# Level products of a gated linear attention in pairs of 64 by 64 blocks, in the two column halves of the array

## The chip, the cores and the metric

The kernel is written in Bass for Trainium2 and runs on one core of one chip. The metric is the time of one execution on the device, in microseconds (us); of several runs the median counts. Everything is fp32.

## The reference, cut to what matters

Two layers of an encoder run over 768 tokens (one sequence of 512 and one of 256). Each layer has a gated linear attention branch (4 heads, 128 key channels, 256 value channels each) and a grouped-query attention branch behind one common input projection. The change touches the first branch alone:

```python
def step(S, inp):                      # one chunk of 64 tokens, forward; the backward one is its mirror, strict
    qi, ki, vi, gi = inp
    b = jnp.cumsum(gi, axis=2)
    diff = b[:, :, :, None, :] - b[:, :, None, :, :]
    decay = jnp.exp(jnp.where(mask[None, None, :, :, None], diff, -jnp.inf))
    A = jnp.einsum('bhic,bhjc,bhijc->bhij', qi, ki, decay)
    o = (jnp.einsum('bhij,bhjv->bhiv', A, vi)
         + jnp.einsum('bhic,bhcv->bhiv', qi * jnp.exp(b), S))
```

Over the whole sequence this is one matrix A over pairs of tokens (i, j), in which each entry is a sum over channels of query times key times the product of the gates between j and i, forward above and backward below the diagonal, and then A times the values.

## The kernel before, in words

The kernel does not walk through chunks. It builds A level by level. On level `span` (`LEVELS` = 1, 2, 4, ... 256) the tokens are cut into blocks of `span`; queries and keys carry the product of the gates up to the border of their block, and the product of the two is A for the pairs of tokens that lie in two neighbouring blocks with a common parent. Doubling the span multiplies queries and keys by the totals of their blocks (`doubled`, L1681 to L1697, on VectorE), and `merge_k` (L1053, ScalarE) picks, for each block, the forward or the backward keys into `scaled[:, 4]`.

For one head `gla_levels` of TensorE (L703) runs `GLA_STEPS` = 10 steps. Step 0 is the plain product of queries and keys (the diagonal), step n the level `LEVELS[n - 1]`. On steps 1 to 7 (spans 1 to 64) it issues one matmul for each of the `NT` = 6 tiles of 128 tokens: the 128 channels are contracted, the stationary side is the 128 keys of the tile, and the moving side is the 128 queries of the tile, of which forward and backward rows of `scaled` alternate in runs of `span` (the three-dimensional `view` on L726). The result is a block of 128 by 128 in PSUM, six beside each other in banks 0 and 1. VectorE then copies into `amat` what lies under the level's mask (`collect`, L1700 with `copy_predicated` on L1706); for spans 1 to 32 the mask is zero in the two corners of the tile that join its first 64 tokens with its last 64, because a pair of blocks of these spans is at most 64 tokens wide. Spans 128 and 256 join different tiles and have their own outputs (`aoff1`, `aoff2`).

Around the levels lies other work of TensorE: `background` (L565) takes tiles of the input projection that are due later, one after the other, with three fp32r matmuls each (L584 to L586, 128 stationary, 256 moving columns). `GLA_DONE` says how many tiles are done by the end of which step; they fill the time in which VectorE and ScalarE prepare the next level. TensorE waits on `prod_free` (VectorE has copied the last product), `k_ready` and `q_ready` before each step, and signals `prod` with the last matmul of a step. ScalarE and GpSimd split the weights for the background into a high and a low part (L935, L1425), and SyncE loads them. After the last level `gla_values` multiplies A with the values (L742). Three heads run in a loop and the last one apart, in each of the two layers, so eight heads in all.

Of the kernel before, what the change touches and what calls it, by code (L numbers as in the profile page):

```python
# [40 lines left out]
P = 128  # L41
# [3 lines left out]
TOK = sum(SEQS)  # L45
# [10 lines left out]
GATE_NORM = 16.0  # L56
LEVELS = (1, 2, 4, 8, 16, 32, 64, 128, 256)
NMASK = 7
AH, KVH, DH = 16, 4, 64
GROUP = AH // KVH  # L60
GRID_W, ROPE_THETA = 64, 10000.0
# [269 lines left out]
def trunk(nc, x_prompt, x_sample, norm_g, w_in, w_gate_f, b_gate_f, w_gate_b, b_gate_b, gla_norm_g,  # L331
          q_norm_g, k_norm_g, w_branch_a, w_branch_b, w_out, final_norm_g,
          identity, masks, rope_cos, rope_sin, y_prompt, y_sample):
    def sb(name, shape, offset, dtype=F32):
        return nc.alloc_sbuf_tensor_at(name, shape, dtype, offset=offset)

    def view(t, start, *dims):

        row = 1
        for n in t.shape[1:]:  # L340
            row *= n
        return bass.AP(t, start, [[row, P]] + [list(d) for d in dims])
# [38 lines left out]
    y_out = sb("y_out", [P, NT, D], R_ACT)  # L381
    mask_raw = sb("mask_raw", [P, NMASK, P], R_O + 13 * ROW)

# [3 lines left out]
    scaled = sb("scaled", [P, 5, TOK], R_O + 6 * ROW)  # L387
# [24 lines left out]
    st_qk = sb("st_qk", [P, 4, NSTAT], R_O + 14 * ROW + NTP * 2 * P * 4)  # L412
    g_qk = sb("g_qk", [P, 2, DH], R_S + P * 4 + NMASK * P + 2 * NSTAT * 4)
    rot1 = sb("rot1", [P, HALF], R_T)
# [3 lines left out]
    ident = sb("ident", [P, P], R_S)  # L418
    mask = sb("mask", [P, NMASK, P], R_S + P * 4, U8)
    st = sb("st", [P, 5, NSTAT], R_S + P * 4 + NMASK * P)  # L420
    bg = sb("bg", [P, 2, GH], R_S + P * 4 + NMASK * P + 5 * NSTAT * 4)
    bg_fix = sb("bg_fix", [P, 2], R_S + P * 4 + NMASK * P + 5 * NSTAT * 4 + 32)
    ps = nc.alloc_psum_tensor("ps", [P, 8 * HALF], F32)
# [47 lines left out]
    with nc.Block() as block:  # L471
# [61 lines left out]
        def _(pe):  # L533
            at = Counts("tensor", pe, w_lo_done=RING, drained=8, pt_lo_ready=2, rot2_free=2)
            mm = nc.tensor.matmul
# [29 lines left out]
            def background(start, stop, bank0=BG_BANK, spare=0, ends=False, turned=0):  # L565


                for u in range(start, stop):
                    i, t = divmod(u, NT)
                    k = i % KT  # L570
                    if t == 0:
                        pe.wait_ge(s.w_lo_done, at("w_lo_done"))
                    end = t == NT - 1
                    if i == 0:
                        t = (t + turned) % NT
                    if turned and u == NT - turned:
                        pe.wait_ge(s.drained, at.peek("drained", 0))
                    if k == 0 and t % 2 == 0:
                        pe.wait_ge(s.bg_free, at.peek("bg_free", 1 - 3 * spare))
                        at.skip("bg_free", 1)  # L580
                    out = ps[:, bank0 * HALF + t * BGW:bank0 * HALF + (t + 1) * BGW]
                    tok = slice(t * P, (t + 1) * P)

                    mm(out, act_hi[:, k, tok], w_hi[:, k % RING, 0:BGW], start=(k == 0 and t % 2 == 0), stop=False, skip_group_check=True)  # L584
                    mm(out, act_hi[:, k, tok], w_lo[:, k % RING, 0:BGW], start=False, stop=False, skip_group_check=True)  # L585
                    last = mm(out, act_lo[:, k, tok], w_hi[:, k % RING, 0:BGW], start=False, stop=(k == KT - 1), skip_group_check=True)  # L586
                    if end:
                        last.then_inc(s.w_used, 1)
                    elif ends and k == KT - 1 and t % 2 == 1:
                        last.then_inc(s.bg_done, 1)  # L590
# [103 lines left out]
            def gla_gates():  # L694

                pe.wait_ge(s.gla_fix, at("gla_fix"))
                pe.wait_ge(s.o_read, at("o_read"))
                for d, start, n in ((0, 0, HALF), (0, HALF, TOK - HALF), (1, 0, TOK - HALF), (1, TOK - HALF, HALF)):
                    z = 2 * HALF + d * TOK + start
                    last = mm(ps[:, z:z + n], wg_fix[:, d, :], gl_t[:, start:start + n], start=True, stop=True)  # L700
                last.then_inc(s.gate_ready, 1)

            def gla_levels(h, done, more):  # L703
                for n in range(GLA_STEPS):
                    pe.wait_ge(s.prod_free, at("prod_free"))
                    if n != 1:
                        pe.wait_ge(s.k_ready, at("k_ready"))
                    if n > 0:
                        pe.wait_ge(s.q_ready, at("q_ready"))

                    span = LEVELS[max(n - 1, 0)]
                    if span == 256:
                        for j in range(NTP):
                            i0, of = (2 * P, 0) if j < 2 else (0, 1)
                            last = mm(ps[:, j * 2 * P:(j + 1) * 2 * P], scaled[:, 4, j * P:(j + 1) * P],
                                      scaled[:, of, i0:i0 + 2 * P], start=True, stop=True)
                    else:
                        for j in range(NT):
                            lhs = scaled[:, 4, j * P:(j + 1) * P]
                            if n == 0:  # L720
                                rhs = view(qk_t, h * (2 * TOK) + j * P, (1, P))
                            elif span == 128:
                                i = j ^ 1
                                rhs = scaled[:, j % 2, i * P:(i + 1) * P]
                            else:
                                rhs = view(scaled, TOK + j * P, (2 * span, P // (2 * span)), (span - TOK, 2), (1, span))  # L726
                            last = mm(ps[:, j * P:(j + 1) * P], lhs, rhs, start=True, stop=True)  # L727
                    last.then_inc(s.prod, 1)
                    background(done[n - 1] if n else GLA_FIRST, done[n])
                    if more and n == GATE_STEP:  # L730
                        gla_gates()
# [121 lines left out]
            for layer in range(DEPTH):  # L853
# [19 lines left out]
                with at.repeat(GH - 1, "gla head") as h:  # L873
                    gla_levels(h, GLA_DONE, True)
                    pe.wait_ge(s.gate_used, at("gate_used", 2))
                    gla_values(h)
                gla_levels(GH - 1, GLA_DONE, False)
                gla_values(GH - 1)
                phase_end(pe, at, s.pe_phase, free=True)
# [1143 lines left out]
```

## Time and profile before

| | us |
|---|---|
| median of 3 runs | 1978.19 |
| lowest and highest run | 1978.09, 1978.83 |
| the profiled execution | 1978.54 |
| its span on the core | 1976.7 |
| mean granted clock of TensorE | 0.995 of full speed |

The profile is of one execution. It gives for each engine its instructions with start and duration. The engines are PE (TensorE's matmuls), PEld (TensorE's weight loads, which overlap matmuls), DVE (VectorE), ACT (ScalarE), POOL (GpSimd) and SP (SyncE). Ends of matmuls are modelled, and their records overlap, so that a stretch is best read from the starts. An fp32 matmul appears as two records of PE and two of PEld; an fp32r matmul appears as one of each, although both are labelled f32. "128*128" before a shape is the part of the array that the instruction uses, as rows by columns. L12 is line 12 of the kernel.

### The profile page before, as it was taken

What the parts mean: (1) busy time and instruction counts of PE and PEld (TensorE: products, weight loads), DVE (VectorE), ACT (ScalarE), POOL (GpSimd) and SP (SyncE); (2) the same over time, 40 slices, a digit from 0 to 9 for tenths busy, and PEclk for the clock granted to TensorE, in tenths of its full rate; (3) what the DMA queues carried; (4) which work ended last, traced back from release to release, by engine and by line L of the source; (5) the groups of instructions that cost most, each with busy time, mean ns of one, the idle gap of its engine ahead of it and who ended that gap; (6) DMA issues with size and microseconds to landing.
All of it is one profiled execution on the core that took longest, in us unless ns stands there. A gap on an engine that the chain in (4) does not pass through costs nothing.

```text
span 1976.7 us, 34929 instructions
## 1 busy us (share of the span) xinstructions
PE 1925.5 (97%) x12944; PEld 1783.0 (90%) x12944; DVE 980.1 (50%) x1376; ACT 943.0 (48%) x1891; POOL 674.9 (34%) x688
## 2 busy tenths in 40 slices
PE   7999999999999999999999999999999999999997
PEld 6989999999999998888899899999999999988886
DVE  5113555569755553434250145557696555643334
ACT  4214554533676775523441335555337767753334
POOL 3423122148311222333653322222672221133244
PEclk9999999999999999999999999999999999999999
DMA  5322221432111114332442122225221121261323
GB/s 173 86 56 58 66 74 53 153 98 61 57 46 60 53 50 161 109 123 70 136 105 66 48 67 63 64 72 164 82 60 49 46 67 44 72 197 64 118 92 143
DMA packets 122961, 169.45 MB, mean 86 GB/s; under 512 B 15696, under 2 KB 89296, under 8 KB 122832
## 3 DMA queue, kind: packets, MB, share of 16 engines
q1 hardware_dynamic: 82656, 107.52, 18.9%
q10 hardware_dynamic: 40176, 60.18, 8.9%
q8 instruction: 85, 1.39, 0.3%
q14 instruction: 44, 0.36, 0.1%
HBM read 136.19 MB, written 31.46 MB: 85 GB/s over the span
## 4 chain that ended last, share of the span: by engine, by line
PE 90%; DVE 3%; ACT 2%; issue 1%; ACTq 1%; DMA 1%; POOL 0%; DVEq 0%
PE ps L584 12%; PE ps L585 12%; PE ps L586 12%; PE ps L538 11%; PE ps L540 10%; PE ps L539 10%; PE ps L727 5%; PE ps L742 3%; PE ps L781 3%; PE ps L795 2%; PE ps L668 2%; PE ps L796 2%; PE ps L770 2%; PE ps L771 2%; ACTq L976 1%
## 5 line engine op out<-in xcount | busy, mean ns | idle before, releaser
L1425 POOL TENSOR_TENSOR w_lo<-w_raw,w_hi 128x256 fp32r<-128x256 f32 (+1 forms) x560 | 570.6, 1026 | 1257.8 <-ACT w_hi L935 1256.1
L584 PE MATMUL ps<-w_hi,act_hi 128*128 128x256 f32 x2112 | 609.8, 289 | 1.9 <-issue 1.3
L586 PE MATMUL ps<-w_hi,act_lo 128*128 128x256 f32 x2112 | 597.2, 283 | 0.0
L585 PE MATMUL ps<-w_lo,act_hi 128*128 128x256 f32 x2112 | 597.2, 283 | 0.0
L935 ACT ACTIVATE w_hi<-w_raw 128x256 fp32r<-128x256 f32 (+1 forms) x560 | 273.4, 495 | 512.3 <-PE ps L540 277.3
L584 PEld LDWEIGHTS ps<-w_hi,act_hi 128*128 128x128 f32 x2112 | 404.0, 191 | 7.5 <-issue 4.1
L585 PEld LDWEIGHTS ps<-w_lo,act_hi 128*128 128x128 f32 x2112 | 404.4, 191 | 2.2
L586 PEld LDWEIGHTS ps<-w_hi,act_lo 128*128 128x128 f32 x2112 | 404.1, 191 | 0.0
L1832 DVE TENSOR_REDUCE st<-ps 128x1 f32<-128x512 f32 (+1 forms) x160 | 109.9, 691 | 126.5 <-PE ps L771 125.9
L538 PE MATMUL ps<-w_hi,o_hi 128*128 128x512 f32 x384 | 155.7, 405 | 1.7 <-DVE merged L1754 0.5
L540 PE MATMUL ps<-w_hi,o_lo 128*128 128x512 f32 x384 | 151.0, 393 | 0.0
L539 PE MATMUL ps<-w_lo,o_hi 128*128 128x512 f32 x384 | 150.9, 393 | 0.0
L1058 ACT ACTIVATE scaled<-scaled 128x768 f32<-128x768 f32 x64 | 53.3, 832 | 154.0 <-DVE scaled L1690 154.0
L1144 ACT ACTIVATE pr<-ps,st 128x512 f32<-128x512 f32 (+1 forms) x192 | 117.1, 612 | 11.8 <-DVE st L1832 9.5
L1838 DVE TENSOR_TENSOR pt_lo<-ps,pt_hi 128x512 fp32r<-128x512 f32 x128 | 88.2, 689 | 60.5 <-ACT pt_hi L1154 59.2
L1154 ACT ACTIVATE pt_hi<-ps 128x512 fp32r<-128x512 f32 x128 | 76.5, 598 | 66.6 <-PE ps L796 51.8
L1706 DVE COPY_PREDICATED amat<-mask,ps 128x768 f32<-128x768 uint8 x56 | 58.0, 1036 | 95.8 <-issue 74.4
L727 PE MATMUL ps<-scaled 128*128 128x128 f32 x768 | 102.4, 284 | 2.0 <-issue 2.0
L781 PE MATMUL ps<-ident,pr 128*128 128x128 f32 x640 | 96.7, 273 | 7.7 <-DVE q_hl L1823 6.9
L727 PEld LDWEIGHTS ps<-scaled 128*128 128x128 f32 x768 | 96.9, 192 | 2.6 <-issue 2.3
L538 PEld LDWEIGHTS ps<-w_hi,o_hi 128*128 128x128 f32 x384 | 72.8, 189 | 19.1 <-issue 3.6
L540 PEld LDWEIGHTS ps<-w_hi,o_lo 128*128 128x128 f32 x384 | 72.8, 190 | 15.9
(181 smaller groups left out, 3468.7 us busy)
## 6 DMA issues: line engine op xcount, KB each, us to landing
w_raw<-in_w_in SPq DMA_DIRECT2D x352, 128.0 KB, 2.1
proj<-stg ACTq DMA_DIRECT2D x36, 768.0 KB, 3.4
w_raw<-in_w_in SPq DMA_DIRECT2D x80, 256.0 KB, 2.7
w_raw<-in_w_out SPq DMA_DIRECT2D x64, 256.0 KB, 2.7
w_raw<-in_w_branch_a SPq DMA_DIRECT2D x32, 256.0 KB, 2.8
w_raw<-in_w_branch_b SPq DMA_DIRECT2D x32, 256.0 KB, 2.7
q<-proj ACTq DMA_DIRECT2D x8, 768.0 KB, 4.8
zb<-proj ACTq DMA_DIRECT2D x8, 768.0 KB, 9.9
```

What stands on the lines that cost most here:

```text
L538: mm(out, s_hi, m_hi, start=first, stop=False)
L539: mm(out, s_hi, m_lo, start=False, stop=False)
L540: return mm(out, s_lo, m_hi, start=False, stop=last)
L584: mm(out, act_hi[:, k, tok], w_hi[:, k % RING, 0:BGW], start=(k == 0 and t % 2 == 0), stop=False, skip_group_check=True)
L585: mm(out, act_hi[:, k, tok], w_lo[:, k % RING, 0:BGW], start=False, stop=False, skip_group_check=True)
L586: last = mm(out, act_lo[:, k, tok], w_hi[:, k % RING, 0:BGW], start=False, stop=(k == KT - 1), skip_group_check=True)
L727: last = mm(ps[:, j * P:(j + 1) * P], lhs, rhs, start=True, stop=True)
L781: last = nc.tensor.transpose(bank(pt_bank(n))[:, place * P:(place + 1) * P], pr[:, n % 2, j * P:(j + 1) * P], ident[:])
L935: A(w_hi[:, slot, 0:width], w_raw[:, slot, 0:width], ACT.Copy).then_inc(s.w_hi_done, 1)
L1144: last = A(pr[:, n % 2, i * w:(i + 1) * w], ps[:, n % 2 * HALF + i * w:n % 2 * HALF + (i + 1) * w], ACT.Exp, bias=nmax(n, i), accum_out=de ...
L1425: G.tensor_tensor(w_lo[:, slot, 0:width], w_raw[:, slot, 0:width], w_hi[:, slot, 0:width].bitcast(F32), ALU.subtract).then_inc(s.w_lo_done, 1)
L1832: V.tensor_reduce(out, view_ps(n % 2 * HALF, (HALF // k, k), (1, HALF // k)), AX.X, ALU.max, negate=True).then_inc(s.neg_max, 1)
```

## The change

Steps 1 to 6 (spans 1 to 32) no longer compute whole tiles. For each chunk of 64 tokens they issue one matmul with the chunk's 64 keys as the stationary and its 64 queries as the moving side. The result goes to the 64 partitions of PSUM that belong to the chunk's place in its tile, 0 to 63 for an even chunk and 64 to 127 for an odd one, so that even chunks use the first 64 columns of the array and odd ones the last 64. The two corners that join the chunks are not computed; PSUM keeps there what it held, and the mask leaves it out of `amat`. The signal, the waits, the other steps and all other engines are as before. From here on line numbers of the change are higher by 1 behind the constant, and by 6 behind the new branch.

```diff
@@ -56,6 +56,7 @@
 LEVELS = (1, 2, 4, 8, 16, 32, 64, 128, 256)
 NMASK = 7
+CHUNK = 64
@@ -714,7 +715,7 @@
                                       scaled[:, of, i0:i0 + 2 * P], start=True, stop=True)
-                    else:
+                    elif n == 0 or span >= CHUNK:
                         for j in range(NT):
                             lhs = scaled[:, 4, j * P:(j + 1) * P]
@@ -725,6 +726,11 @@
                                 rhs = view(scaled, TOK + j * P, (2 * span, P // (2 * span)), (span - TOK, 2), (1, span))
                             last = mm(ps[:, j * P:(j + 1) * P], lhs, rhs, start=True, stop=True)
+                    else:
+                        for c in range(0, TOK, CHUNK):
+                            rows = slice(c % P, c % P + CHUNK)
+                            rhs = view(scaled, TOK + c, (2 * span, CHUNK // (2 * span)), (span - TOK, 2), (1, span))
+                            last = mm(ps[rows, c:c + CHUNK], scaled[:, 4, c:c + CHUNK], rhs, start=True, stop=True)
                     last.then_inc(s.prod, 1)
```

In the program of TensorE the six matmuls of such a step become twelve. The rows below are those of step 4 (span 8) in the looped heads, before; REGISTER_ALU is the count for a wait, L700 the gates of the next head:

```order
L700 MATMUL ps<-gl_t,wg_fix 128x512
L705 REGISTER_ALU
L707 REGISTER_ALU
L727 MATMUL ps<-scaled 128x128 x6
L584 MATMUL ps<-w_hi,act_hi 128x256
L585 MATMUL ps<-w_lo,act_hi 128x256
L586 MATMUL ps<-w_hi,act_lo 128x256
```

and the same place now:

```order
L701 MATMUL ps<-gl_t,wg_fix 128x512
L706 REGISTER_ALU
L708 REGISTER_ALU
L733 MATMUL ps<-scaled 64x64 x12
L585 MATMUL ps<-w_hi,act_hi 128x256
L586 MATMUL ps<-w_lo,act_hi 128x256
L587 MATMUL ps<-w_hi,act_lo 128x256
```

Nothing else has moved: the same work stands before and behind the products on TensorE, and every other engine has the same rows with new line numbers.

## Rows read from the trace of the kernel before

**Rows 1.** The page, part 1: busy time, share of the span, instructions of each engine.
```profile
PE 1925.5 (97%) x12944; PEld 1783.0 (90%) x12944; DVE 980.1 (50%) x1376; ACT 943.0 (48%) x1891; POOL 674.9 (34%) x688
```

**Rows 2.** The page, part 4: the chain that ended last, by engine and line.
```profile
PE 90%; DVE 3%; ACT 2%; issue 1%; ACTq 1%; DMA 1%; POOL 0%; DVEq 0%
```

**Rows 3.** Busy time by stretch: the first head of each layer.
```profile
core 0: us, PE busy (x) PEld busy (x) DVE busy (x) ACT busy (x) POOL busy (x), PEclk, DMA share, GB/s
183.00:241.70 58.70, 58.67 (x450) 57.15 (x450) 30.94 (x38) 27.07 (x41) 13.54 (x19) 1.00 0.24 77
1158.00:1216.50 58.50, 58.48 (x450) 56.95 (x448) 30.94 (x38) 26.85 (x40) 13.55 (x19) 1.00 0.25 78
```

**Rows 4.** The chain in order of time, 184 to 209 us: start, us, what.
```profile
184.76 2.00 PE ps L727 x12
190.71 1.45 PE ps L727 x12
196.11 1.34 PE ps L727 x12
...
202.11 1.34 PE ps L727 x12
207.39 1.34 PE ps L727 x12
```

**Rows 5.** Instructions of line 727 on PE and PEld: duration ns min/median/max, start of first and last.
```profile
L727 PEld LDWEIGHTS ps<-scaled x768: 186/192/196, 184.5 to 1374.8; 128*128 128x128 f32 x192
L727 PE MATMUL ps<-scaled x768: 271/275/348, 184.6 to 1374.9; 128*128 128x128 f32 x192
```

**Rows 6.** Timeline of PE, 201 to 203.6 us: start, us, engine, line, operation, tiles.
```profile
201.00 0.28 PE L585 MATMUL ps<-w_lo,act_hi 128*128 128x256 f32 x1
201.12 0.28 PE L586 MATMUL ps<-w_hi,act_lo 128*128 128x256 f32 x1
...
201.95 1.50 PE L727 MATMUL ps<-scaled 128*128 128x128 f32 x12
203.20 0.36 PE L584 MATMUL ps<-w_hi,act_hi 128*128 128x256 f32 x1
203.40 0.28 PE L585 MATMUL ps<-w_lo,act_hi 128*128 128x256 f32 x1
203.52 0.28 PE L586 MATMUL ps<-w_hi,act_lo 128*128 128x256 f32 x1
```

**Rows 7.** Timeline of PE, 227 to 230 us: the products of span 256.
```profile
227.98 1.89 PE L715 MATMUL ps<-scaled 128*128 128x256 f32 x8
```

**Rows 8.** Timeline of PEld, 129.8 to 132.6 us, past a drain in the program.
```profile
130.79 0.19 PEld L538 LDWEIGHTS ps<-w_hi,act_hi 128*128 128x128 f32 x1 [0.65 <-issue]
130.90 0.19 PEld L539 LDWEIGHTS ps<-w_lo,act_hi 128*128 128x128 f32 x1
```

**Rows 9.** Timeline of PE over the same place.
```profile
129.94 0.39 PE L539 MATMUL ps<-w_lo,act_hi 128*128 128x512 f32 x1
130.17 0.39 PE L540 MATMUL ps<-w_hi,act_lo 128*128 128x512 f32 x1
130.82 0.47 PE L538 MATMUL ps<-w_hi,act_hi 128*128 128x512 f32 x1 [0.26 <-DVE va L1920]
```

**Rows 10.** Timeline of PEld, 564.4 us: two weight loads of transposes; then 564.65, one alone.
```profile
564.38 0.20 PEld L781 LDWEIGHTS ps<-ident,pr 128*128 128x128 f32 x2 [0.49 <-ACTq L1146]
564.65 0.14 PEld L781 LDWEIGHTS ps<-ident,pr 128*128 128x128 f32 x1
```

**Rows 11.** Timeline of all engines, 186.9 to 190.6 us, between two levels.
```profile
186.90 1.03 DVE L1706 COPY_PREDICATED amat<-mask,ps 128x768 f32<-128x768 uint8 x1 [2.47 <-PE ps L727]
187.82 0.94 DVE L1690 TENSOR_TENSOR scaled<-scaled,gate 128x768 f32<-128x768 f32 x1
188.80 0.96 ACT L1058 ACTIVATE scaled<-scaled 128x768 f32<-128x768 f32 x1 [4.13 <-DVE scaled L1690]
190.54 0.29 PE L727 MATMUL ps<-scaled 128*128 128x128 f32 x1
```

**Rows 12.** Waits of PE for others, longest first.
```profile
PE ps L727 <- issue: 2.0, 2, 1.2
```

## The prediction

> **What bounds the kernel now.** I read the page's busy times first: the matmuls fill 97% of the span, VectorE 50%, ScalarE 48% [rows 1]. Then the chain that ended last, where TensorE holds 90% [rows 2]. Both say that a saving on TensorE is a saving of time, and an addition an addition. The change lies in one stage, so I asked for that stage by itself: in one head of the linear attention TensorE is busy 58.67 of 58.70 us in the first layer and 58.48 of 58.50 in the second, at the full granted clock, which is the 2.4 GHz level, while VectorE has 31 us of work and ScalarE 27 [rows 3]. In all eight heads together PE stood idle ahead of line 727 for 2.0 us, at two places of 1.2 us at most [rows 12]. So here TensorE is the bound almost to the last nanosecond, and the time that the changed matmuls hold it is what counts.
>
> **What the changed part costs now.** The chain in order of time shows the groups of line 727 of one head: twelve records each, 2.00 us for span 1, 1.45 for span 2, 1.34 for each of spans 4 to 32 [rows 4]; the row for span 32 is like those of 4 to 16. That makes 2.00 + 1.45 + 4 x 1.34 = 8.81 us per head and 70.5 us over eight heads: the most that is at stake. Six matmuls give twelve records, since an fp32 matmul is two.
>
> How long a record holds the engine is read from starts, since its duration of 275 ns [rows 5] is its whole way through the array. The group at 201.95 us lasts 1.50 us; without the last record's 0.275 that leaves 11 spacings, 0.1114 us each [rows 6]. With 256 moving columns (eight records in 1.89 us, the last of them some 0.38 us) the spacing is (1.89 - 0.38) / 7 = 0.216 us [rows 7]. Hence 128 columns cost 0.1046 us and each record a constant 0.0068. Two things run at this pace side by side: the moving columns, and the weight loads. Behind a drain, with nothing in their way, two loads of 128 columns start 0.11 us apart [rows 8]. So both the stream and the loads are at their limit in line 727, and for a gain the change must relieve both.
>
> **The change, part by part.**
>
> 1. *Half the stationary columns, half the moving ones, twice the matmuls.* A group becomes 24 records with 64 moving columns and loads of 64. If they go one after the other, a record takes 0.0523 + 0.0068 = 0.059 us, and a group 24 x 0.059 = 1.42 us in place of 1.34: +0.082 us, times 48 groups (6 steps x 4 heads x 2 layers) **+3.9 us**. The loads alone need half of 0.11 us each, 24 x 0.055 = 1.32 us, so they give the same answer even if the streams of the two halves ran at once. I take this value. What was thrown away was arithmetic, and no row says that the array charges for arithmetic: it charges for columns streamed and columns loaded, and 24 x 64 is 12 x 128. The corners cost moving columns only if the halves really work beside each other; that is the rival.
>
> 2. *Twelve more instruction pairs per group.* Can TensorE issue a matmul and a load every 0.055 us? At 564.38 two loads fill 0.20 us, of which the second takes 0.14, so it starts 0.06 us behind the first, with a matmul issued between them [rows 10]. If 0.06 were the floor, 24 pairs would take 1.44 us, 0.02 over the 1.42; that is +1 us in all. From below the floor costs nothing. I leave it at nothing.
>
> 3. *Switching between the whole array and its halves.* Every group is now entered from matmuls on 128*128 and left for them: 96 switches. The trace of before has none; every record is 128*128. Bounds: below, nothing, since the change from fp32r to fp32 and back at 201.95 leaves no gap: the sequence from 201.95 to the second background matmul at 203.40 is 1.45 us for twelve spacings of 0.1114 and one of 0.12 [rows 6]. Above, the drain that the program itself orders: from the start of L540 at 130.17 to that of L538 at 130.82 is 0.65 us where two of its kind stand 0.23 apart, so 0.42 us for each, part of which is a semaphore [rows 9]; 96 x 0.42 = 40 us. What a switch that only has to let the array run empty would cost lies between: a background matmul lasts 0.28 us and its successor starts 0.12 us behind it, so 0.16 us are its tail [rows 6], which a drain exposes; and if the weight load may not go ahead either, half of 0.11 us on the way in and 0.11 on the way out come on top [rows 8]. That is 2 x 0.16 = 0.32 to 0.49 us per group. I take 0.40, because loads run ahead everywhere else: 48 x 0.40 = **+19.2 us**. The value is nearest to the tail, which is a row, and far from 0, because I suppose that results still on their way through one cut of the array have to leave it before another cut is set.
>
>    The Trainium skill states the rule outright (TensorEngine Tiling (Array Packing), Key Properties): changing the tiling mode drains TensorE, changing only the tile does not. By that rule the 96 switches are paid and the steps from one half to the other inside a group are free; without it the sum would be 3.9 us.
>
> 4. *The other engines.* VectorE's masked copy, its products and ScalarE's `merge_k` are as before. Their chain starts with the product's signal (L1706 at 186.90) and ends at 188.80 + 0.96 = 189.76, while TensorE comes back at 190.54 after a fixed amount of background [rows 11]. That 0.78 us of slack does not depend on how long the group took, so neither a shorter nor a longer group turns into a wait. The one place where TensorE waits 1.2 us in each layer [rows 12] stays or absorbs up to as much, 2 us in all, which I don't count.
>
> Sum: 3.9 + 0 + 19.2 = +23.1 us on the profiled execution's 1978.54, so 2001.6; that execution stands 0.35 us above the median of 1978.19, so against the median **2001.3 us**, 1.2% slower. A measurement of this kernel can tell about 0.2% (4 us) from no change. The forecast's own range comes from the tail alone (3.9 + 15.4: 1997.5) to tails with both loads (3.9 + 23.5: 2005.6), with a little for item 2: 1996 to 2008.
>
> **The rivals.**
>
> *A. The halves work at once, and switches are paid (faster).* If loads and streams of an even and an odd chunk overlap fully, a group takes half of what it takes in item 1: the 70.5 + 3.9 us become 37.2, a saving of 33.3 us. With the 19.2 us of switches 14.1 us are left: 1964 us. It decides against my forecast from the point where the saving passes 0.40 us a group, that is where a pair of 64-column records takes less than about (1.34 - 0.40) / 12 = 0.078 us. For it: the code alternates the halves, and the two write different partitions. Against it: a load of 128 columns takes 0.11 us by itself [rows 8], and if two loads of 64 share what feeds them, they take the same. The Trainium skill promises up to twice the speed where the stationary side has at most 64 columns, and lets different tiles load and multiply in parallel (TensorEngine Tiling (Array Packing), Theoretical Speedup and Key Properties). The Trainium skill also says that loads overlap matmuls in flight only when the row group differs (TensorE: Matmul & The Clock Gate, Part 3), and here it never does; no row of before can show either.
>
> *B. The halves work at once, and switches are free (faster).* 33.3 us saved: 1945 us. It needs both a mechanism that no row shows and the absence of the one that item 3 prices.
>
> *C. One after the other, and switches are free (no change or a hair slower).* The change then does not do what its name says: pairs in two halves, but no pair at once. +3.9 us: 1982 us; without the constant per record 1978.
>
> *D. Dearer switches (slower).* The drain as the program orders it, 0.42 us each: 3.9 + 40: 2022 us, or a pair of instructions that needs more than 0.07 us.
>
> **How the numbers follow.** The forecast has 0.40, A 0.22, B 0.13, C 0.17, D 0.08. Slower by over 0.2%: the forecast, D, and the share of C that lies past 4 us (0.04), 0.52. Within 0.2%: the rest of C, 0.13. Faster by over 0.2%: A and B, 0.35. The range reaches from A with somewhat dearer switches (33.3 saved, 15 paid: from 1960) to the top of the forecast (2008); it leaves out B and D, 0.21 in all. The forecast's own range is 1996 to 2008.
>
> **What the profile of the changed kernel would show.** Line 733 with 1152 records of form 128*64 (24 in each of 48 groups). Item 1: records of a group about 0.055 to 0.06 us apart, alike from half to half; under A pairs of starts much closer together, and a group under 0.8 us. Item 3: a gap of 0.15 to 0.3 us between the start of the last background matmul plus its 0.12 and the first record of line 733, and another behind the last; under C or B none. Item 4: the masked copy still waits for TensorE, and PE's idle ahead of the group stays near 2 us. A head would grow from 58.7 us to about 61.6, under A shrink to about 56.9. The prediction is wrong in kind if a group of spans 4 to 32, from the end of background spacing to its resumption, takes less than 1.34 us, and wrong in size if the two gaps together are not 0.3 to 0.5 us.

## The result, and the profile after

The changed kernel takes 1962.64 us (median of 4 runs, 1962.20 to 1963.97) against 1978.51 for the kernel before: 15.9 us less, a ratio of 0.992 with a 95% interval of 0.9903 to 0.9937. So it is faster, clear of the 0.2% that can be told. The forecast of 2001.3 us was wrong in sign; the time is that of rival A (1964 us), in which the two halves of the array work at once and the switches are paid. One run further down, of the kernel with the even chunks first, took 3168.07 us at a mean granted clock of 0.557, where every other run in this document has 0.993 to 0.997; it is left out of that kernel's median.

The page of the changed kernel, parts 1 and 4 (answers to [rows 1, 2]):

```profile
PE 1907.5 (97%) x13520; PEld 1754.9 (89%) x13520; DVE 987.3 (50%) x1376; ACT 942.8 (48%) x1891; POOL 680.0 (35%) x688
...
PE 88%; DVE 4%; ACT 3%; issue 3%; ACTq 1%; DMA 0%; POOL 0%; DVEq 0%
```

TensorE has 576 more matmul records and 18 us less to do; the busy times of the other engines are within 1% of what they were. Busy time by stretch of the first head (answers to [rows 3]; the head now ends 2.1 us sooner):

```profile
core 0: us, PE busy (x) PEld busy (x) DVE busy (x) ACT busy (x) POOL busy (x), PEclk, DMA share, GB/s
183.00:239.60 56.60, 56.27 (x523) 53.52 (x522) 30.97 (x38) 27.05 (x41) 13.57 (x19) 1.00 0.25 80
```

The changed matmuls by themselves, duration ns min/median/max (answers to [rows 5]):

```profile
L733 PEld LDWEIGHTS ps<-scaled x1152: 132/138/143, 184.8 to 1347.3; 128*64 128x64 f32 x192
L733 PE MATMUL ps<-scaled x1152: 222/222/288, 184.8 to 1347.3; 128*64 128x64 f32 x192
```

There are twice as many records, of the form 128*64. Now the decisive view: the timeline of PE around the group of span 4.

```profile
194.77 0.28 PE L586 MATMUL ps<-w_lo,act_hi 128*128 128x256 f32 x1
194.89 0.28 PE L587 MATMUL ps<-w_hi,act_lo 128*128 128x256 f32 x1
195.09 0.92 PE L733 MATMUL ps<-scaled 128*64 128x64 f32 x24
195.94 0.39 PE L585 MATMUL ps<-w_hi,act_hi 128*128 128x256 f32 x1
196.16 0.28 PE L586 MATMUL ps<-w_lo,act_hi 128*128 128x256 f32 x1
```

24 records fill 0.92 us. One after the other at my 0.059 us they would fill 23 x 0.059 + 0.222 = 1.58. Where the window is cut down to the first hundredths of a microsecond of the group, the timeline of PE and of PEld shows why:

```profile
195.09 0.28 PE L733 MATMUL ps<-scaled 128*64 128x64 f32 x2
...
195.09 0.14 PEld L733 LDWEIGHTS ps<-scaled 128*64 128x64 f32 x2
```

Two loads together last 0.14 us, and a single one has a median of 0.138 in the rows above; two matmuls last 0.28, and the first alone 0.27. By unrounded starts the second of each pair begins some 7 ns behind the first, and they run side by side. A group is therefore 12 slots, and not 24. The slot follows from the block: 0.92 less the last record's 0.222, less 0.05 by which the first slot is longer than the rest, less the 7 ns by which the last record trails its partner, leaves 11 slots, 0.058 us each.

The rest of a group's time is the two switches. From the last background matmul at 194.89 to the second one behind the group at 196.16 are 1.27 us; two ordinary background spacings of 0.12 belong to the background, so the group costs 1.03 us (1.04 by unrounded starts). Twelve slots are 0.70; the other 0.34 are a first start 0.09 late and a first slot 0.05 long on the way in, and 0.20 on the way out: the background's first matmul starts 0.10 behind the end of the slots, and its successor 0.22 behind it in place of 0.12. (In the kernel before the successor stood 0.20 behind it too [rows 6], but there the first had started 0.08 before the spacings of the group were over, so that nothing was lost.) The weight loads show more of the way in. Timeline of PEld, the kernel before and the changed one, at the start of the group of span 4:

```profile
195.71 0.19 PEld L586 LDWEIGHTS ps<-w_hi,act_lo 128*128 128x128 f32 x1
195.83 0.31 PEld L727 LDWEIGHTS ps<-scaled 128*128 128x128 f32 x2
...
194.77 0.19 PEld L587 LDWEIGHTS ps<-w_hi,act_lo 128*128 128x128 f32 x1
195.09 0.14 PEld L733 LDWEIGHTS ps<-scaled 128*64 128x64 f32 x2
```

Before, the load of the group's first keys starts 0.12 us behind the load ahead of it and 0.11 us ahead of its own matmul (195.94). Now it starts 0.32 us behind the load ahead of it, in the same hundredth of a microsecond as its own matmul (195.09). So at a switch the load does not run ahead. On the way out it is the same: the background's first load and first matmul both start at 195.94.

The chain in order of time has the other spans (answers to [rows 4]; a piece of the chain begins some 0.06 us behind the group's first record):

```profile
184.82 1.15 PE ps L733 x24
190.12 0.90 PE ps L733 x24
195.16 0.85 PE ps L733 x24
```

Reckoned from starts in the same way, switches included, the groups of a head cost 1.35 us for span 1, 1.09 for span 2 and 1.04 for each of the other four, where they cost 2.00, 1.45 and 1.34: 2.2 us less a head, 17.7 us over eight heads. That is more than the 15.9 us between the medians, and the waits of PE show where to look for the rest:

```profile
PE ps L585 <- ACT stg L956: 2.5, 8, 0.3
...
PE ps L728 <- issue: 2.4, 2, 1.2
```

The background's first matmul behind span 16 waits, in each of the six looped heads, for ScalarE to copy previous sums out of PSUM (`stg`). The page of before has 0.5 us of such waits, at two other places, and 2.5 now. But the 2.0 us between them are not what was lost, for the background waited here before as well. The first copy and the background's first matmul behind it, before and after:

```profile
208.11 1.57 ACT L950 ACTIVATE stg<-ps 128x512 f32<-128x512 f32 x3
208.76 0.39 PE L584 MATMUL ps<-w_hi,act_hi 128*128 128x256 f32 x1
...
206.40 1.57 ACT L956 ACTIVATE stg<-ps 128x512 f32<-128x512 f32 x3
207.04 0.39 PE L585 MATMUL ps<-w_hi,act_hi 128*128 128x256 f32 x1 [0.33 <-ACT stg L956]
```

Both times the matmul starts 0.65 us behind the start of the copy. Before, that was 0.30 us behind the last record of the group, where 0.03 is usual; the wait hid under the modelled end of that record, and so the page does not list it among PE's waits. By starts the place cost 0.29 us a head before and costs 0.41 now, 0.7 us more over six heads. The waits ahead of the products in the last heads (spans 32 and 64 before, nearly all on span 64 now: 2.4 against 2.0 on the page) cost 0.6 us more by starts. Hence 17.7 - 0.7 - 0.6 = 16.4 us at the groups, against 15.9 between the medians and 14.6 between the two profiled executions.

### The profile page after: what moved, and what is told of

The parts are those of the page before. It is cut to its first block, busy times and chain, and to the rows that moved or that the text cites. A ratio compares the mean times of both kernels' runs of the same rounds, so it can differ in the third digit from the quotient of the medians.

```text
span 1962.2 us, 36081 instructions
## 1 busy us (share of the span) xinstructions
PE 1907.5 (97%) x13520; PEld 1754.9 (89%) x13520; DVE 987.3 (50%) x1376; ACT 942.8 (48%) x1891; POOL 680.0 (35%) x688
## 3 DMA queue, kind: packets, MB, share of 16 engines
q8 instruction: 87, 1.43, 0.3%
## 4 chain that ended last, share of the span: by engine, by line
PE 88%; DVE 4%; ACT 3%; issue 3%; ACTq 1%; DMA 0%; POOL 0%; DVEq 0%
PE ps L585 12%; PE ps L586 11%; PE ps L587 11%; PE ps L539 11%; PE ps L541 10%; PE ps L540 10%; PE ps L748 4%; PE ps L787 3%; PE ps L669 2%; PE ps L801 2%; PE ps L802 2%; PE ps L733 2%; PE ps L776 2%; PE ps L728 2%; PE ps L777 2%
## 5 line engine op out<-in xcount | busy, mean ns | idle before, releaser
L1431 POOL TENSOR_TENSOR w_lo<-w_raw,w_hi 128x256 fp32r<-128x256 f32 (+1 forms) x560 | 577.3, 1037 | 1238.3 <-ACT w_hi L941 1237.3
L539 PEld LDWEIGHTS ps<-w_hi,o_hi 128*128 128x128 f32 x384 | 73.0, 190 | 19.2 <-issue 3.6
L541 PEld LDWEIGHTS ps<-w_hi,o_lo 128*128 128x128 f32 x384 | 72.8, 190 | 15.9
L539 PE MATMUL ps<-act_hi,w_hi 128*128 128x384 f32 x256 | 86.2, 337 | 0.6 <-DVE qk_t L1641 0.6
L541 PE MATMUL ps<-act_hi,w_lo 128*128 128x384 f32 x256 | 85.6, 334 | 0.0
```

What stands on the lines that cost most here:

```text
L539: mm(out, s_hi, m_hi, start=first, stop=False)
L541: return mm(out, s_lo, m_hi, start=False, stop=last)
L1431: G.tensor_tensor(w_lo[:, slot, 0:width], w_raw[:, slot, 0:width], w_hi[:, slot, 0:width].bitcast(F32), ALU.subtract).then_inc(s.w_lo_done, 1)
```

## The experiments

Theory 1 is that of the trace: each column half streams and loads by itself, so two blocks take the time of one, and a way into the halves and out again costs 0.34 us. (The halves can't be told here from the two sets of PSUM partitions that they write.) Its rival, theory 2, is that nothing runs at once and a small record is simply cheap. The first four kernels were compared with the kernel before at 1978.33 us on the same chip, the later ones with 1978.29 and 1978.88; the changed kernel had been compared with 1978.51, so differences to it are good to some 0.6 us, beside the spread of the runs.

**Even chunks first.**

```diff
-                        for c in range(0, TOK, CHUNK):
+                        for c in [*range(0, TOK, P), *range(CHUNK, TOK, P)]:
```

> The same twelve matmuls per group, but the six even chunks first and then the six odd ones, so that neighbours in the program lie in the same column half. Theory 1 (the two halves load and stream at once, and this needs neighbours in different halves): 24 slots of 0.058 us follow each other in place of 12, a group takes 1.74 us in place of 1.04, +33 us over 48 groups, about 1996 us. Theory 2 (nothing runs at once, a 64 by 64 record is simply cheap, about 0.03 us): no change from the changed kernel, 1963 us.

Measured: 1983.82 us (median of 5 runs, 1982.75 to 1985.29), ratio 1.0031 (1.0018 to 1.0044). Timeline of PE around the group of span 4:

```profile
194.28 0.28 PE L587 MATMUL ps<-w_hi,act_lo 128*128 128x256 f32 x1
194.49 1.43 PE L733 MATMUL ps<-scaled 128*64 128x64 f32 x24
195.86 0.38 PE L585 MATMUL ps<-w_hi,act_hi 128*128 128x256 f32 x1
196.08 0.28 PE L586 MATMUL ps<-w_lo,act_hi 128*128 128x256 f32 x1
```

The same twelve matmuls with the same records last 1.43 us in place of 0.92, and the group costs 1.56. Theory 2 falls: the work is the same and only the neighbours differ. Theory 1 holds in its direction, not in its size. (1.43 - 0.222 - 0.05) / 0.058 = 20 slots behind the first, 21 in all, where strictly one after the other would be 24: three slots held two records. By unrounded starts the first odd record begins at 0.52 us, when three of the even half's twelve have still to start. So the odd half begins before the even one is through, but only a few records ahead. The alternation of the halves in the program is worth 21.2 us.

**Halves, but nothing skipped.**

```diff
                         for c in range(0, TOK, CHUNK):
                             rows = slice(c % P, c % P + CHUNK)
-                            rhs = view(scaled, TOK + c, (2 * span, CHUNK // (2 * span)), (span - TOK, 2), (1, span))
-                            last = mm(ps[rows, c:c + CHUNK], scaled[:, 4, c:c + CHUNK], rhs, start=True, stop=True)
+                            t = c - c % P
+                            rhs = view(scaled, TOK + t, (2 * span, P // (2 * span)), (span - TOK, 2), (1, span))
+                            last = mm(ps[rows, t:t + P], scaled[:, 4, c:c + CHUNK], rhs, start=True, stop=True)
```

> Pairs in the two halves as in the change, but each chunk of 64 keys meets all 128 queries of its tile, so that the corners are computed again. Theory 1: a pair of records takes what one whole-array record took, 12 slots of 0.111 us, and the switches of 0.34 us per group stay: 16 us above the kernel before, about 1995 us. It would show that the halves alone bring nothing and that the saving is the skipped corners, which only the halves make payable. Theory 2: 24 records of 128 moving columns one after the other, 2.7 us a group, about 2058 us.

Measured: 1993.39 us, ratio 1.0075 (1.0055 to 1.0095), 15.1 us above the kernel before, 0.31 us per group; by starts, too, a group of span 4 costs 1.65 us against 1.34. Timeline of PE, span 4:

```profile
196.55 0.28 PE L587 MATMUL ps<-w_hi,act_lo 128*128 128x256 f32 x1
196.76 1.53 PE L734 MATMUL ps<-scaled 128*64 128x128 f32 x24
198.22 0.39 PE L585 MATMUL ps<-w_hi,act_hi 128*128 128x256 f32 x1
```

24 records of 128 moving columns last 1.53 us, as twelve did on the whole array (1.50, [rows 6]). So a half has the full pace for itself, and the halves by themselves bring nothing but the bill for the switches. The saving is the corners that are skipped. Arithmetic that is thrown away is paid as streamed columns; the halves are what makes it possible not to stream them. Theory 2, with 2058 us, falls here as well.

**Chunks of queries against whole tiles of keys.** Tiles of 64 moving columns on the whole array, no halves; nothing is skipped.

```diff
-                            rows = slice(c % P, c % P + CHUNK)
+                            t = c - c % P
                             rhs = view(scaled, TOK + c, (2 * span, CHUNK // (2 * span)), (span - TOK, 2), (1, span))
-                            last = mm(ps[rows, c:c + CHUNK], scaled[:, 4, c:c + CHUNK], rhs, start=True, stop=True)
+                            last = mm(ps[:, c:c + CHUNK], scaled[:, 4, t:t + P], rhs, start=True, stop=True)
```

> The queries are cut in chunks of 64, the keys are not: 24 records per group on the whole array, 128 columns loaded and 64 streamed, no switch. If the weight loads bind (0.11 us for 128 columns), a group takes 24 x 0.111 = 2.66 us in place of 1.34, +64 us: about 2042 us. If only the streamed columns bind, 24 x 0.059 = 1.42 us: about 1982 us.

Measured: 2033.91 us, ratio 1.028 (1.0259 to 1.03). Timeline of PE, span 1:

```profile
184.40 0.28 PE L587 MATMUL ps<-w_hi,act_lo 128*128 128x256 f32 x1
184.52 2.81 PE L733 MATMUL ps<-scaled 128*128 128x64 f32 x24
```

(2.81 - 0.28) / 23 = 0.110 us a record, though half as many columns stream: the weight loads bind. The expected 2042 took 1.34 us for the old cost of every group, but span 1 had cost 2.00 and span 2 1.45; six groups of 24 x 0.111 = 2.66 us against 8.81 are 57 us over eight heads, 2036 us. This is the part of item 1 that was right: stream and loads run side by side, each at its limit, and both must shrink. In the changed kernel both do. The group also starts 0.12 us behind the last background matmul, as it did before: 24 small records on the whole array pay no way in, so the gap of the changed kernel belongs to the halves.

**Twice the switches.**

```diff
                     else:
                         for c in range(0, TOK, CHUNK):
+                            if c == TOK // 2:
+                                background(done[n - 1], done[n - 1] + 1)
...
-                    background(done[n - 1] if n else GLA_FIRST, done[n])
+                    background(done[n - 1] + (n > 0 and span < CHUNK) if n else GLA_FIRST, done[n])
```

> The changed kernel with the first background tile of each step moved between the first six and the last six products of its group: the same matmuls, but four switches between whole array and halves per group in place of two. If a way in and a way out together cost 0.34 us, as the starts in the changed kernel's trace say: +16 us, about 1979 us, all of the gain gone. If the gaps around a group are something else (the start of the group, the waits on VectorE and ScalarE), they don't double: 1963 us.

Measured: 1982.89 us, ratio 1.0025 (1.0015 to 1.0034), 20.3 us above the changed kernel. Timeline of PE, span 4:

```profile
193.72 0.28 PE L587 MATMUL ps<-w_hi,act_lo 128*128 128x256 f32 x1
193.93 0.57 PE L735 MATMUL ps<-scaled 128*64 128x64 f32 x12
194.43 0.39 PE L585 MATMUL ps<-w_hi,act_hi 128*128 128x256 f32 x1
194.65 0.28 PE L586 MATMUL ps<-w_lo,act_hi 128*128 128x256 f32 x1
194.77 0.28 PE L587 MATMUL ps<-w_hi,act_lo 128*128 128x256 f32 x1
194.98 0.57 PE L735 MATMUL ps<-scaled 128*64 128x64 f32 x12
```

and its waits for the copies out of PSUM and ahead of the products:

```profile
PE ps L585 <- ACT stg L958: 7.2, 10, 1.0
...
PE ps L728 <- issue: 1.0, 2, 0.8
```

The same gap of 0.21 us stands before either half of the group, 0.09 more than between two background matmuls. 4.7 us of the 20.3 are more waiting for `stg` than in the changed kernel, and 1.4 us less are lost ahead of the products (1.0 against 2.4). The 17.0 that remain are 0.35 us for each of the 48 added ways in and out. By starts the two halves of the group of span 4 cost 0.69 us each, 1.38 together against 1.04, so 0.34. The price of a switch is shown twice, by the starts and by doubling it.

**Span 64 in halves.**

```diff
-                    elif n == 0 or span >= CHUNK:
+                    elif n == 0 or span > CHUNK:
...
+                            if span == CHUNK:
+                                to = c ^ CHUNK
+                                rhs = scaled[:, c // CHUNK % 2, to:to + CHUNK]
...
+                            last = mm(ps[rows, to:to + CHUNK], scaled[:, 4, c:c + CHUNK], rhs, start=True, stop=True)
```

> The changed kernel with span 64 in halves too: its products are the two corners of each tile, twelve 64 by 64 blocks, and the two diagonal blocks are left out. Theory 1: 8 more groups go from 1.34 to 1.04 us, -2.4 us, about 1960 us, less if the shorter groups turn into waits for free PSUM in the background, as the changed kernel shows 2 us of. If new waits eat all of it: 1963 us.

Measured: 1960.69 us (1957.24 to 1963.40), ratio 0.9913 (0.9898 to 0.9928). The median is 2 us below the changed kernel, but the runs overlap with its own, so the times alone show nothing. By starts a group of span 64 in a looped head costs 1.04 us in place of 1.34, as expected, but PE's idle ahead of the products grew to 3.8 us, from 2.4 in the changed kernel:

```profile
PE ps L731 <- issue: 3.8, 3, 1.6
```

**Quarters for spans 1 to 16.**

```diff
-                        for c in range(0, TOK, CHUNK):
-                            rows = slice(c % P, c % P + CHUNK)
-                            rhs = view(scaled, TOK + c, (2 * span, CHUNK // (2 * span)), (span - TOK, 2), (1, span))
-                            last = mm(ps[rows, c:c + CHUNK], scaled[:, 4, c:c + CHUNK], rhs, start=True, stop=True)
+                        size = max(2 * span, 32)
+                        for c in range(0, TOK, size):
+                            rows = slice(c % P, c % P + size)
+                            rhs = view(scaled, TOK + c, (2 * span, size // (2 * span)), (span - TOK, 2), (1, span))
+                            last = mm(ps[rows, c:c + size], scaled[:, 4, c:c + size], rhs, start=True, stop=True)
```

> The changed kernel with blocks of 32 by 32 in the four column quarters for spans 1 to 16, 24 matmuls a group; span 32 stays at 64 by 64. Theory 1 carried on (four quarters at once): 12 slots of 0.033 us in place of 0.058, 0.30 us less in each of 40 groups, -12 us, about 1951 us. If instructions can't be issued faster than one per 7 ns, as the starts of a pair stand apart, four loads and four matmuls need 56 ns a slot and nothing is gained: about 1963 us. Slower than that if the issue floor is higher.

Measured: 1952.94 us, ratio 0.988 (0.9865 to 0.9895), 9.7 us below the changed kernel. Timeline of PE, span 4:

```profile
193.87 0.28 PE L587 MATMUL ps<-w_hi,act_lo 128*128 128x256 f32 x1
194.08 0.63 PE L734 MATMUL ps<-scaled 128*32 128x32 f32 x48
194.64 0.39 PE L585 MATMUL ps<-w_hi,act_hi 128*128 128x256 f32 x1
194.87 0.28 PE L586 MATMUL ps<-w_lo,act_hi 128*128 128x256 f32 x1
```

48 records in 0.63 us, the last of them 0.196. By unrounded starts the first eight slots of four records are 0.032 us apart (behind a first one of 0.05), so that issuing four loads and four matmuls in 0.03 us is no floor there. But the last 16 records no longer start in fours, and the group ends 0.05 us later than at that pace, so that a slot is 0.04 us on the average ((0.63 - 0.196) / 11). What holds the last records is open; a limit of issuing that shows only once the first 32 pairs are through is not excluded. The group costs 194.87 - 193.87 - 0.24 = 0.76 us, of which more than 0.3 are still the switches. By starts the groups of spans 1 to 16 cost 13.6 us less than in the changed kernel, waits left out; 9.7 are measured: PE now waits 4.5 us for `stg` and 3.7 ahead of line 728, 3.3 more than in the changed kernel.

```profile
PE ps L585 <- ACT stg L957: 4.5, 10, 0.6
PE ps L728 <- issue: 3.7, 2, 2.4
```

**Both together.** The edits of the last two: quarters for spans 1 to 16, halves for 32 and 64.

> The two that gained put together: 32 by 32 blocks in quarters for spans 1 to 16, 64 by 64 blocks in halves for span 32, and the two corner blocks in halves for span 64. If the savings add: 1953 us less the 2 us that span 64 gave by itself, about 1951 us. If shorter groups now only turn into waits for VectorE and ScalarE (3.7 us of idle ahead of the products stand in the quarters' trace already): 1953 us.

Measured: 1948.78 us (1948.47 to 1952.15), ratio 0.9854 (0.9838 to 0.9871). It is the fastest of all, 30.1 us below the kernel before and 13.9 below the changed kernel; its runs lie below those of the quarters alone (1952.49 to 1956.53). Busy time by stretch of its first head:

```profile
181.00:236.00 55.00, 54.40 (x656) 51.62 (x655) 31.26 (x38) 27.20 (x41) 13.64 (x19) 1.00 0.26 83
```

TensorE idles 0.6 us of the 55, where it idled 0.03 of 58.7 [rows 3].

## Why the prediction was right or wrong

**What bounds the kernel** held: TensorE fills 97% before and after, and what its products cost is what the kernel gained, save for 1.3 us of waits. "Almost to the last nanosecond" was too much: behind span 16 the background already waited 0.29 us a head, which the busy share hides, as the modelled ends of the records before reach over it.

**Item 1 failed, and with it the forecast and its direction.** It put the 24 records one after the other, 1.42 us a group, on the ground that the loads alone need 24 x 0.055 us. The price of a load was right (the whole-array experiment found the loads to bind at 0.110), and so was the slot, 0.059 forecast and 0.058 measured. Wrong was the step from "a load of 128 columns takes 0.11 us" to "two loads of 64 share what feeds them". No row of before could carry it, since every record there used the whole array. The trace after shows two loads in the time of one, so a group has 12 slots: 0.70 us in place of 1.42, and with the switches 1.04, below the 1.34 that the prediction had named as the sign of being wrong in kind. In the prediction this stood under rival A as the argument against it, at a chance of 0.22.

The Trainium skill had both sides. That different tiles load and multiply in parallel (TensorEngine Tiling (Array Packing), Key Properties) agrees with this trace: loads and matmuls start 7 ns apart in pairs. The trace agrees in its outcome with the rule of the same section that item 3 names as well: entering and leaving the halves costs 0.34 us, and a step from one half to the other inside a group nothing. That a load overlaps a matmul in flight only with another row group (TensorE: Matmul & The Clock Gate, Part 3), which I counted against A, does not: all records here use all rows, and in one half a load and the other half's matmul overlap throughout.

**Item 2** held: twelve more pairs of instructions cost nothing. In the quarters, with 48 pairs a group, the first 32 did not either; for the last 16 it is open.

**Item 3** was right in kind and nearly in size: 0.40 us a group forecast, 0.34 measured, 16.3 us in all in place of 19.2. But its pieces were not those of the prediction, so part of that nearness is luck. It took 0.16 us of tail at either end, and left the loads out "because loads run ahead everywhere else". The trace shows 0.14 on the way in and 0.20 on the way out, and loads that do not run ahead of a switch. The group starts 0.21 us behind the start of the last background matmul, whose record lasts 0.28; since ends are modelled, this can't decide whether results have to leave the array first. The drain that the program orders, 0.42 for one switch, was far too dear, and "nothing" too cheap. By these numbers the change would bring about 32 us instead of 16 if the switches were free.

**Item 4** was wrong by 1.3 us. It looked at the chain from one product to the next, with 0.78 us of slack, and in the looped heads no new wait appeared there. It overlooked the other thing that TensorE waits for: the copies that free PSUM for the background. The copy behind span 16 starts by ScalarE's work and not by the length of that group, and the background, which waited for it before, now reaches it sooner (0.7 us). The rest (0.6 us) is ahead of the products in the last heads, whose waits in the kernel before were 1.2 us in one layer and 0.7 in the other, and not 1.2 in each.

**The rivals.** A (1964 us) is what happened, by its mechanism, with 34.0 us saved in the slots (forecast 33.3), 16.3 paid in switches (19.2) and 1.3 in waits (0); that makes 16.4, where 15.9 were measured. B fails on the switches, C on the halves that do work at once, D on both. The threshold given under A, a pair of records below 0.078 us, was met with 0.058. The range of 1960 to 2008 did hold 1962.6, but only because it had been stretched down to A; the forecast's own, 1996 to 2008, did not. Its lower end stands for cheaper switches than the forecast's (15 us against 19.2), not for dearer ones, as the prediction words it.

## What to carry to other kernels

A matmul that fills a part of its output with what a mask throws away can be cut into blocks for separate column parts of the array, if it is limited by its streamed columns and weight loads: here two blocks in two halves took the time of one, and four blocks of 32 by 32 in four quarters took 0.032 us a slot where two of 64 by 64 took 0.058, for the first 32 records of a group. Neighbours in the program have to alternate between the parts, and nothing was gained without skipping something (a half had the pace of the whole array, not more). Each group pays about a third of a microsecond for the way in and out, so it must save more than that. And a wait is read best from starts: the page lists only what the modelled end of the matmul ahead does not cover. Whether groups of the same cut put together would save switches was not tried.

## What the runs showed of the hardware that was not expected

Two column halves run loads and matmuls at once at the full pace of each, 0.058 us for a pair of fp32 records with 64 columns, and four quarters do so at 0.032 us for the first 32 of 48 records, 0.04 on the average of the group. Going from the whole array to halves and back costs 0.34 us by starts (0.35 by doubling it), and 0.3 to 0.4 us for quarters; at such a switch the weight load does not start ahead of its matmul. With all even blocks ahead of all odd ones, 24 records took 21 slots, so the second half starts only a few records early.
